# Keys and values of the projection turned by VectorE in 32 by 32 blocks and by the stores' address patterns

## What is computed

```python
h = rmsnorm(x, g_norm)                              # x_prompt: (1, 2048, 1024)
proj = jnp.einsum('bld,de->ble', h, w_in)           # w_in: (1024, 10240)
u_p, z_p, q, k, v, z_r, gates = jnp.split(proj, IN_SPLITS, axis=-1)
...
def retention_chunk(q, k, v, s, log_gamma):         # 4 heads; q, k 256 wide, v 512 wide
    scores = jnp.einsum('bhid,bhjd->bhij', q, k) * decay[None]
    inner = jnp.einsum('bhij,bhjv->bhiv', scores, v)
    cross = jnp.einsum('bhid,bhdv->bhiv', q_dec, s)
    s_new = jnp.exp(log_gamma * C)[None, :, None, None] * s + jnp.einsum('bhjd,bhjv->bhdv', k_dec, v)
```

## Time and profile before

| | |
|---|---|
| median of 3 runs | 2834.74 us (2834.27 to 2839.41) |
| the profiled execution | 2833.37 us |
| its span in the profile | 2831.6 us |
| busy: PE, DVE, ACT, POOL | 2782.2, 1808.3, 1126.4, 684.8 us |
| mean granted TensorE clock | 0.997 of 2.4 GHz |
| moved by DMA | 552.8 MB, 195 GB/s |

### The profile page before, as it was taken

One profiled execution on the slowest core, in us unless ns is written; L12 is line 12 of the kernel. 1 busy time (PEld: TensorE's weight loads), 2 busy tenths in 40 slices (PEclk: granted clock), 3 DMA queues, 4 the chain that ended last, 5 costly groups with the idle time before them and its releaser, 6 DMA issues.

```text
span 2831.6 us, 36714 instructions
## 1 busy us (share of the span) xinstructions
PE 2782.2 (98%) x13504; PEld 2249.1 (79%) x13504; DVE 1808.3 (64%) x2588; ACT 1126.4 (40%) x1901; POOL 684.8 (24%) x456
## 2 busy tenths in 40 slices
PE   6999999999999999999999999999999999999998
PEld 5888888888877777777777787877887888788876
DVE  8667566667555365655755566676677667766775
ACT  5444444444554444443434433333333333333332
POOL 5253433434332223425334330000000000000000
PEclk9999999999999999999999999999999999999999
DMA  4544444454564344453444458487648764876496
GB/s 144 197 146 155 173 147 158 156 179 145 180 223 153 113 156 162 147 186 125 163 154 154 165 200 307 141 278 289 246 145 283 289 239 150 283 290 234 153 340 261
DMA packets 281849, 552.80 MB, mean 195 GB/s; under 512 B 24216, under 2 KB 166872, under 8 KB 270527
## 3 DMA queue, kind: packets, MB, share of 16 engines
q1 hardware_dynamic: 266279, 541.73, 53.5%
q10 hardware_dynamic: 15168, 8.46, 1.0%
q0 software_dynamic: 224, 0.26, 0.0%
HBM read 375.59 MB, written 175.14 MB: 194 GB/s over the span
## 4 chain that ended last, share of the span: by engine, by line
PE 90%; DVE 4%; DMA 2%; issue 2%; ACT 1%; POOL 0%; ACTq 0%; SPq 0%; DVEq 0%; POOLq 0%
PE bank L1310 28%; PE bank L1312 28%; PE bank L1311 28%; PE bank L1360 2%; PE bank L1383 1%; PE bank L1502 1%; DMA raw<-in_w_branch_ret 1%; DVE w_lo L2173 1%; DVE xa_lo L2173 1%; DVE xs L2187 1%; PE bank L1632 1%; PE bank L1620 0%; PE bank L1610 0%; DMA x_d<-x_out 0%; DMA raw<-in_w_branch_pool 0%
## 5 line engine op out<-in xcount | busy, mean ns | idle before, releaser
L1310 PE MATMUL bank<-xa_hi,wa_hi 128*128 128x512 f32 x2240 | 888.8, 397 | 5.5 <-ACT part_s L1864 3.2
L1312 PE MATMUL bank<-xa_hi,wa_lo 128*128 128x512 f32 x2240 | 873.6, 390 | 0.0
L1311 PE MATMUL bank<-xa_lo,wa_hi 128*128 128x512 f32 x2240 | 873.5, 390 | 0.0
L1310 PEld LDWEIGHTS bank<-xa_hi,wa_hi 128*128 128x128 f32 x2240 | 420.6, 188 | 107.8 <-issue 21.5
L1312 PEld LDWEIGHTS bank<-xa_hi,wa_lo 128*128 128x128 f32 x2240 | 420.5, 188 | 90.0
L1311 PEld LDWEIGHTS bank<-xa_lo,wa_hi 128*128 128x128 f32 x2240 | 421.1, 188 | 82.8
L2173 DVE TENSOR_TENSOR wa_lo<-w_raw,wa_hi 128x512 fp32r<-128x512 f32 x320 | 312.7, 978 | 165.9 <-ACT wa_hi L1857 165.1
L2173 DVE TENSOR_TENSOR wa_lo<-w_sum,wa_hi 128x512 fp32r<-128x512 f32 x240 | 194.2, 809 | 241.3 <-ACT wa_hi L1857 241.3
L2173 DVE TENSOR_TENSOR w_lo<-raw,w_hi 128x512 fp32r<-128x512 f32 (+1 forms) x288 | 181.9, 659 | 189.3 <-ACT w_hi L1971 189.2
L1857 ACT ACTIVATE wa_hi<-w_raw 128x512 fp32r<-128x512 f32 x320 | 201.2, 629 | 242.6 <-PE bank L1312 238.3
L1971 ACT ACTIVATE w_hi<-raw 128x512 fp32r<-128x512 f32 (+1 forms) x288 | 166.4, 603 | 306.6 <-PE bank L1312 208.5
(11 more groups left out here) (253 smaller groups left out, 4311.8 us busy)
## 6 DMA issues: line engine op xcount, KB each, us to landing
w_raw<-in_w_in SPq DMA_DIRECT2D x80, 1024.0 KB, 5.3
v_d<-turned SPq DMA_DIRECT2D x64, 512.0 KB, 3.2
qk_s<-qk_d SPq DMA_DIRECT2D x32, 1024.0 KB, 7.4
v_s<-v_d SPq DMA_DIRECT2D x32, 1024.0 KB, 11.5
raw<-in_w_branch_ret SPq DMA_DIRECT2D x128, 256.0 KB, 4.2
tabs<-in_c_rope SPq DMA_DIRECT2D x16, 1024.0 KB, 6.9
qk_d<-high SPq DMA_DIRECT2D x32, 512.0 KB, 4.6
qk_d<-c_low SPq DMA_DIRECT2D x32, 512.0 KB, 5.4
```

The costliest lines, as they stand in the source:

```text
L1310: pe.matmul(out, lh, rh, start=first, stop=False, skip_group_check=onto)
L1311: pe.matmul(out, lh, rl, start=False, stop=False, skip_group_check=onto)
L1312: return pe.matmul(out, ll, rh, start=False, stop=last, skip_group_check=onto)
```

## The change

Transposes on TensorE for keys and values go away. VectorE instead transposes each 128x512 tile in blocks of 32 by 32 (turn_blocks, two instructions for each half of the tokens, at i = 0 and i = 2 of the next job): values in place in c_out, keys into tabs, the place of the rope tables. That leaves the blocks themselves at the wrong partitions; the stores put them right with their address patterns, one DMA for each group of 32 partitions (BA = 4), and for keys one for each of the high and low halves too. A stored piece is 256 bytes for keys and 512 for values, where it was 4096 and 1024. To make pieces of two blocks, the columns of value jobs are taken in an interleaved order (weight_columns), and the features of the keys lie in an interleaved order in scratch; so the rotated queries and keys are stored in that order too, in 4 DMAs instead of one, and the final states likewise. turn_high and turn_low read SBUF instead of a PSUM bank. Loads of the second phase take two pieces for each partition instead of one.

The weight sums of GpSimd, and the high and low halves of weights, go through the same interleaved pattern for value jobs (not shown). Two new functions, keys_of_chunk and values_of_chunk, make the loads (not shown).

```diff
+BT = 32
+BA = P // BT
...
-        kt_d = scratch("kt_d", [NB, HEADS, NC, P, 2, 2, DK])
-        v_d = scratch("v_d", [NB, HEADS, NC, P, 2, 2, DV])
+        kt_d = scratch("kt_d", [NB, HEADS, NT, P, 2, BA, 2 * BT])
+        v_d = scratch("v_d", [NB, HEADS, NT, P, 2, BA, 4 * BT])
...
+                if kind(i) == "k":
+                    engine.wait_ge(turn_lo, 4 * before(i + 1, "k", "v"))
 
         def stores(j):
 
-            return {"q": 64, "k": 64, "v": 0}.get(kind(j), 32)
+            return {"q": 64 * BA, "k": 64 * BA, "v": 0}.get(kind(j), 32)
 
...
+            if kind(j) == "v":
+                return w.rearrange("p k (a e s) -> p k a e s", a=BA, e=2)[:, :, :, e, :]
+            return w[:, :, e * P:(e + 1) * P]
+
+        def like_weights(j, w):
+
+            return w.rearrange("p k (a s) -> p k a s", a=BA) if kind(j) == "v" else w
...
+
+        def turned_part(j, n, low):
+
+            return turned[:, n % TURNED, :, low]
+
+        def turned_source(j, q):
+
+            t, c = q // 2, q % 2
+            if kind(j) == "v":
+                return c_out[:, j % 2, t, :, c * CHUNK:(c + 1) * CHUNK].rearrange("p e (b s) -> p b e s", s=BT)
+            return tabs[:, c, t * T:(t + 1) * T].rearrange("p (b e s) -> p b e s", b=8, e=2)
 
         def turn_scale(j):
             return float(gamma[JOBS[j][1]] ** CHUNK) if kind(j) == "k" else 1.0
+
+        def turned_stores(n):
+
...
         def turned_free(engine, n):
 
             if n >= 4 * before(NJ, "k", "v"):
                 new_operands(engine, NJ)
             if n >= TURNED:
-                engine.wait_ge(t_stored[n % TURNED], 16 * (n // TURNED))
+                engine.wait_ge(t_stored[n % TURNED], turned_stores(n))
 
         def all_turned_stored(engine, j):
 
             n = 4 * before(j, "k", "v")
             for i in range(TURNED):
...
-                        dst = kt_d[b, i, c] if what == "k" else v_d[b, i, c][:, :, :, part * DK:(part + 1) * DK]
-                        sp.dma_start(dst, turned[:, n % TURNED].bitcast(F32)).then_inc(t_stored[n % TURNED], 16)
+                        for a in range(BA):
+                            src = turned[a * BT:(a + 1) * BT, n % TURNED].bitcast(F32)
+                            if what == "v":
+                                dst = v_d[b, i, 2 * c:2 * c + 2, :, part, a].rearrange("n (b r) x -> r (n b) x", b=BA)
+                                sp.dma_start(dst, src.rearrange("r b h e s -> r b (h e s)"))\
+                                    .then_inc(t_stored[n % TURNED], 16)
+                                continue
+                            for low in range(2):
+                                dst = kt_d[b, i, 2 * c:2 * c + 2, :, low, a].rearrange("n (b r) x -> r (n b) x", b=BA)
+                                sp.dma_start(dst, src[:, :, low].rearrange("r b e s -> r b (e s)"))\
+                                    .then_inc(t_stored[n % TURNED], 16)
                 for t in range(2):
                     b = 2 * (j // NJ) + t
                     out = c_out[:, j % 2, t]
                     if what in ("q", "k"):
                         sp.wait_ge(qk_lo_done, 2 * before(j, "q", "k") + t + 1)
                         dst = qk_d[b, i, "qk".index(what)]
-                        sp.dma_start(dst[:, 0], qk_high[t][:].bitcast(F32)).then_inc(c_stored[j % 2], 16)
-                        sp.dma_start(dst[:, 1], c_low[:, j % 2, t].bitcast(F32)).then_inc(c_stored[j % 2], 16)
+                        for low, src in enumerate((qk_high[t], c_low[:, j % 2, t])):
+                            for a in range(BA):
+                                rows = dst[a % 2 * 2 * BT:(a % 2 + 1) * 2 * BT, low, a // 2]
+                                sp.dma_start(rows.rearrange("(e s) t -> s e t", e=2),
...
-                    sp.dma_start(io["ret_prompt"][0, 0, p].rearrange("(k p) v -> p k v", p=P), state[:, p])\
-                        .then_inc(state_stored, 16)
+                    final = io["ret_prompt"][0, 0, p].rearrange("(e k a s) v -> a e s k v", e=2, k=2, a=2)
+                    for part in range(BA):
+                        sp.dma_start(final[part // 2, part % 2], state[part * BT:(part + 1) * BT, p]).then_inc(state_stored, 16)
...
-            def turn(j, q):
-
-                t = q // 2
-                n = 4 * before(j, "k", "v") + q
-                if kind(j) == "k":
-                    pe.wait_ge(rope_done, 2 * before(j, "q", "k") + t + 1)
-                elif t == 0:
-                    pe.wait_ge(c12_done, j + 1)
-                else:
-                    pe.wait_ge(c21_done, j + 1)
-                if n >= 2:
-                    pe.wait_ge(turn_lo, n - 1)
-                if q == 0:
-                    rides_copied(pe, j + 2)
-                for i in range(2):
-                    tile = 2 * (q % 2) + i
-                    for e in range(2):
-                        mm = pe.transpose(banks[6 + q % 2][:, (2 * i + e) * P:(2 * i + e + 1) * P],
-                                          c_out[:, j % 2, t, e, tile * P:(tile + 1) * P], ident[:])
-                mm.then_inc(turn_mm, 1)
-
             def sample_x():
...
+                        mm = split_product(banks[6 + d][:, :], kt_s[s][:, c, j, 0, w], kt_s[s][:, c, j, 1, w],
+                                           v_s[s][:, c, j, :, 0, :], v_s[s][:, c, j, :, 1, :], j == 0, j == 1)
...
-                act.wait_ge(turn_mm, n + 1)
-                act.activation(turned[:, n % TURNED, 0].rearrange("p i d -> p (i d)"), banks[6 + q % 2][:], ACT.Copy,
-                               scale=turn_scale(j)).then_inc(turn_hi, 1)
+                act.wait_ge(blocks_turned, n - q + 2 * (q // 2) + 2)
+                act.activation(turned_part(j, n, 0), turned_source(j, q), ACT.Copy, scale=turn_scale(j)).then_inc(turn_hi, 1)
...
 
+            def turn_blocks(j, t):
+                if kind(j) == "k":
+                    dve.wait_ge(rope_done, 2 * before(j, "q", "k") + t + 1)
+                elif t == 0:
+                    dve.wait_ge(c11_done, j + 1)
+                    dve.wait_ge(c12_done, j + 1)
+                else:
+                    dve.wait_ge(c21_done, j + 1)
+                    dve.wait_ge(c22_done, j + 1)
+                for e in range(2):
+                    src = c_out[:, j % 2, t, e, :]
+                    if kind(j) == "k":
+                        src = src.rearrange("p (c b s) -> p c b s", c=2, s=BT)
+                    dve.transpose(blocks(j, t, e), src).then_inc(blocks_turned, 1)
+
             def turn_low(j, q):
                 n = 4 * before(j, "k", "v") + q
                 turned_free(dve, n)
                 dve.wait_ge(turn_hi, n + 1)
-                dve.scalar_tensor_tensor(out=turned[:, n % TURNED, 1].rearrange("p i d -> p (i d)"),
-                                         in0=banks[6 + q % 2][:], scalar=turn_scale(j),
-                                         in1=turned[:, n % TURNED, 0].rearrange("p i d -> p (i d)").bitcast(F32),
-                                         op0=ALU.mult, op1=ALU.subtract).then_inc(turn_lo, 1)
+                if kind(j) == "v":
+                    tt(turned_part(j, n, 1), turned_source(j, q), turned_part(j, n, 0).bitcast(F32), ALU.subtract, turn_lo)
+                    return
+                dve.scalar_tensor_tensor(out=turned_part(j, n, 1), in0=turned_source(j, q), scalar=turn_scale(j),
+                                         in1=turned_part(j, n, 0).bitcast(F32), op0=ALU.mult, op1=ALU.subtract)\
+                    .then_inc(turn_lo, 1)
 
             def rope_low(j, t):
                 dve.wait_ge(qk_hi_done, 2 * before(j, "q", "k") + t + 1)
                 if kind(j) == "k":
-                    dve.wait_ge(turn_mm, 4 * before(j, "k", "v") + 2 * t + 2)
+                    dve.wait_ge(blocks_turned, 4 * before(j, "k", "v") + 2 * t + 2)
...
@@ -2358,8 +2406,12 @@
                     if j and kind(j - 1) in ("k", "v") and 2 <= i < 6:
                         turn_low(j - 1, i - 2)
                     weight_low(PROD * j + i + SLOTS)
+                    if j and kind(j - 1) in ("k", "v") and i == 0:
+                        turn_blocks(j - 1, 0)
                     if j and kind(j - 1) in ("q", "k") and i < 2:
                         rope(j - 1, 1, (i,))
+                    if j and kind(j - 1) in ("k", "v") and i == 2:
+                        turn_blocks(j - 1, 1)
```

## The result

The changed kernel takes 2880.7 us (2878.6 to 2883.3), the kernel before in the same comparison 2836.2 (2834.3 to 2839.4): 1.0161 of its time, interval 1.0148 to 1.0174. The change costs 44.5 us. I had predicted 2849, a loss of 15.6 against the profiled execution.

What follows compares the result with a forecast made beforehand. TensorE, 98% busy with 90% of the chain, was taken as the bound. 2833.4 - 45.1 (transposes gone) + 60.4 (waits behind SyncE's small stores) = 2848.7, predicted as 2849 us; range 2796 to 2915.

Steps and rivals of the forecast that it cites:

- the end of SyncE's queue: Job after a key job (start S): SyncE's 48 DMAs take 22.9 us, last lands S+37.95, holding c_out and TensorE.
- TensorE's gain: In TensorE's queue 384 transposes, 96 turns of 0.47 us, go away, saving 45.1 us.
- VectorE: 96 block transposes at 0.60 us add 58 us to VectorE; TensorE waits 1.5 at c22, not added.
- rival "VectorE": Block transposes of 1.2 us move the first store by 1.2 and c22 by 2.4 more; 2873 us, chance 0.10.
- SyncE's pace: Each small store issued right behind another costs SyncE 0.477 us, with ends of 0.365 and 0.56.
- The landing: The last 128 KB store of rotated keys lands about 2.0 us after its issue begins.
- From the landing to TensorE's seventh product: VectorE, once c_out is free, needs 8 starts of 0.60 us and 0.69 for the eviction of c22.
- The clock: TensorE's waits behind key jobs may each bring half clock; taken as 0, range +1.7 x 8 = 14 us.
- Sum of a key job: TensorE's waits lose 8.1 us per key job in the first pass, 7.0 in the second; 60.4 in all.
- The second phase: 64-column operand blocks, half-size loads and 16 end-state DMAs cost nothing; bounds 0 to +15 and 0 to +5 us.
- Cheap issues: Rival: new DMAs cost SyncE 0.365 us each, leaving only the 1.5 wait at c22; 2800 us, chance 0.22.
- Pieces: Rival: a 256-byte store costs 0.040 us, full rings hold SyncE; 2890 us, chance 0.16 shared with few in flight.

Runs made afterwards that it cites:

- e4: Changed kernel with the reordering moved from the stores to the second phase's loads, 20 DMAs a key job instead of 48; 2883.2 us against 2835.8, 1.0167.
- e10: Changed kernel with the same 48 small DMAs a key job, each moving half its elements, the rest left out; 2867.1 us against 2835.8, 1.0104.
- e6: Changed kernel with 24 matmuls into an unused bank ahead of TensorE's wait before the sixth product; 2875.5 us against 2835.9, 1.0136.
- e7: Changed kernel with the 16 stores of rotated keys issued by ScalarE instead of SyncE; 2835.6 us against 2835.9, 0.9997.
- e8: e7 with VectorE's low half of the first rotated keys one step later, behind the addition that frees bank c22; 2826.5 us, 0.9967.
- e1: Changed kernel with only the values turned by VectorE; TensorE turns the keys, stored as before the change; 2811.0 us against 2835.8, 0.9913.

## Why the prediction was off

The sign, the place and the chain were right, and the time lay inside the range (2796 to 2915), but above the 2820 to 2875 that the forecast gave to its own mechanism. Between the two profiled executions the loss was 42.0 in the projection, where I had worked out 15.3, and 4.65 behind it, where I had put nothing.

The step that failed is the end of SyncE's queue. The sum let the last rotated key land at S+37.95, as if the DMA engines were free; it landed at S+39.97 in the first pass and S+40.48 in the second, and c_out, and with it TensorE, was held for that long. That makes 18 of the 28 us that the sum of the key jobs lacked. Some 8 more are the half clock, which the sum put at nothing. Term by term:

- **TensorE's gain: right.** Jobs with turns fell from 20.93 to 19.04, 1.89 in each of 24: 45.4, against 45.1.
- **VectorE: right.** A transpose took 0.69 (0.60 from start to start, as taken); J3 lost 1.28 to 1.30 where 1.5 was worked out. That two-input operations slow beside GpSimd (to 0.86 and 0.99 on average) was named, and had the cover that I named. The rival "VectorE" (2873, closest to the measured time) is refuted by e4's projection, not by the total.
- **SyncE's pace: right for rotated keys, 0.03 low for turned keys.** I took 0.477 from two rows; the trace has 0.505 and 0.477 as medians, and 0.52 and 0.49 as means over the 32 and the 16 (0.54 and 0.49 in the second pass), since single issues took up to 2.0 us. The 0.03 goes with the pieces: with half of them it is gone (e10, 0.474), and rotated keys, with twice the bytes, don't have it. The last issue started at S+36.61 instead of 35.97, although the first was 0.31 early, and at S+37.41 in the second pass. What made the long issues was not traced.
- **The landing: the largest miss.** I took 2.0 us for the last 128 KB, from the fastest landing of a lone store (1.7); it took 3.4 (39.97 - 36.61; 3.1 in the second pass), with the engines 0.92 busy around it. That is 1.4 and 1.1 a key job. e10 shows that the load does it: with half the bytes in it and in the stores ahead, and the load of w_raw just as close behind, the last store landed in 1.9. A landing time belongs to the load around it, and the median (2.6 for line 823) was not the last one's either.
- **From the landing to TensorE's seventh product: 5.8 instead of 5.49** (4.8 + 0.69) where the clock is full (e6, e7, e8), 0.33 more a key job. To the sixth it was 1.72 instead of 1.29 (39.97 to 41.69), spread over the starts of the eviction, the copy and the product; but, as the prediction has it, the seventh is the one that VectorE's chain holds.
- **The clock: taken as 0, with 1.7 a key job as its bound.** From the landing to the seventh product the changed kernel takes 6.87 us in the first pass and 6.70 in the second, where 5.82 are needed at full clock: 1.05 and 0.88, which agrees with e6. The mechanism named, a half clock behind a wait, partly hidden by the wait for c22, is what happened.
- **Sum of a key job, first pass:** 8.1 + 0.64 (issues) + 1.38 (landing) + 0.33 (chain) + 1.05 (clock) = 11.5, against 11.69 measured; in the second pass 7.0 + 1.44 + 1.09 + 0.33 + 0.88 = 10.7, against 10.46. All eight lost 88.6, of which my sum had 60.4: of the 28 missing, some 10 are landing, 8 issues, 8 clock, 3 the chain.
- **The second phase: 4.65 more, taken as nothing between 0 and 5.** At 2764 TensorE waits 2.4 us for VectorE's s_qk (0.7 before), and half clock follows:

```profile
PE bank L1628 <- DVE s_qk L2598: 2.4, 1, 2.4
```

e1 has the same wait (2.5) with the end state stored in one DMA a part, so the four DMAs of the end state are not its cause; what delays it was not isolated. Where the rest of the 4.65 comes from stays open too.
- **Cheap issues (2800): refuted.** In a row they took 0.43 and 0.46 at the median, with 0.04 between them. **Pieces (2890): refuted as a bound, alive as a cost.** A 256-byte store does cost the engines more for its bytes. Queue 1 in a stretch of key stores alone (packets, MB, share of 16 engines over 6 us):

```profile
q1 hardware_dynamic: 3239, 0.78, 73.8%
```

0.738 x 16 x 6 / 3239 = 0.022 us a piece, inside my bounds of 0.009 and 0.030, for half the bytes of the 0.030 pieces, so 1.5 times as much for each byte (the 0.030 is from another queue, under another load). The Trainium skill, DMA: Bandwidth & Descriptors, section Specifications, has such pieces read, modified and written. No run here shows the reading; the trace agrees in that they are dearer for their bytes, but shows no doubling that would hold up SyncE.

## What to carry to other kernels

Count what is behind a DMA twice: the issuing engine's time for each one (0.47 us here, for 32 to 128 KB), and the DMA engines' time for its pieces; where both are close, removing one shows only the small gap to the other. A transpose that goes into address patterns multiplies DMAs on one queue, so ask first what buffer the last of them holds, and take its landing from a row with the same load around it. And read an experiment by stage: one whose total spoke for the wrong theory had won back all the loss in the stage that was in question.

## What the runs showed of the hardware

- A 128x512 block transpose of 4-byte elements on VectorE takes 687 ns, 0.60 from start to start, with or without GpSimd at work beside it.
- Two-input operations on 128x512 took 686 ns with one input in PSUM. With both in SBUF they took 0.67 to 0.69 where GpSimd was idle and 1.27 to 1.31 on average where it worked for more than half of the time; one of the keys' low halves took 1.47.
- A DMA costs SyncE 0.43 us and 0.04 to the next, whether it carries 32 KB of turned keys or 64 or 128 KB of rotated ones; 0.46 with 64 KB in 256-byte pieces; 0.30 as the first behind a wait.
- Two issuers reach 0.95 of the DMA engines; the issues of the turned keys then lengthen from 0.46 to 0.74 us, and their landing from 1.9 to 3.5.
- A TensorE wait of 7.7 us brought the clock from 2.4 to 1.2 GHz until 6.0 us after its end; 24 matmuls inside the wait kept it up in seven of eight cases.
